# Spreading the variance of a LayerNorm over the partitions in one product

## The reference

```python
def layer_norm(x, g, b):
    xf = x.astype(F32)
    mu = jnp.mean(xf, axis=-1, keepdims=True)
    var = jnp.mean(jnp.square(xf - mu), axis=-1, keepdims=True)
    return ((xf - mu) * lax.rsqrt(var + EPS)).astype(x.dtype) * g + b

def conformer_conv(a, gt, w_dw, b_dw, ln_g, ln_b, w_pw):
    y = a * jax.nn.sigmoid(gt)
    y = lax.conv_general_dilated(y, w_dw[:, None, :], window_strides=(1,), ...) + b_dw
    return jax.nn.silu(layer_norm(y, ln_g, ln_b)) @ w_pw
```

## Time and profile before

| | us |
|---|---|
| median of 3 runs | 2111.23 |
| lowest and highest run | 2109.42 and 2115.57 |
| the profiled execution, its own time | 2113.24 |
| its span, first to last instruction | 2111.4 |
| PE busy | 1960.2 (93%) |
| DVE busy | 525.9 (25%) |
| ACT busy | 471.9 (22%) |

### The profile page before, as it was taken

How to read it: one execution, slowest core, us unless ns; L and a number is a source line. 1 busy time by engine, 2 the same in 40 slices (tenths; PEclk the granted TensorE clock), 3 DMA queues, 4 the chain that set the end, 5 groups by cost and what they waited for, 6 DMA issues and landing times.

```text
span 2111.4 us, 36634 instructions
## 1 busy us (share of the span) xinstructions
PE 1960.2 (93%) x15008; PEld 1099.3 (52%) x15008; DVE 525.9 (25%) x1193; ACT 471.9 (22%) x1031; POOL 150.5 (7%) x124
## 2 busy tenths in 40 slices
PE   5999999994999999999979999989879999999995
PEld 3756677882434444343456656778634443434342
DVE  1257122624111110111121841245421111111112
ACT  2232233222212111111131223332321111212112
POOL 0000001000010110101000000000001101011110
PEclk9999899996999999999989999999889999999998
DMA  9213123147899999999943122225449999999997
GB/s 307 84 58 120 41 81 103 68 175 285 327 390 393 385 394 389 390 393 390 388 143 119 64 80 80 68 76 207 171 179 384 392 391 390 392 390 394 386 397 250
DMA packets 210040, 533.78 MB, mean 253 GB/s; under 512 B 17072, under 2 KB 99376, under 8 KB 209712
## 3 DMA queue, kind: packets, MB, share of 16 engines
q1 hardware_dynamic: 191824, 493.52, 61.5%
q0 software_dynamic: 12288, 23.07, 5.1%
q10 hardware_dynamic: 5856, 16.16, 1.9%
HBM read 506.59 MB, written 26.12 MB: 252 GB/s over the span
## 4 chain that ended last, share of the span: by engine, by line
PE 68%; DMA 14%; SPq 8%; DVE 4%; issue 3%; ACT 2%; ACTq 0%; DVEq 0%; POOLq 0%
PE wide L1169 13%; DMA ring<-w_up 12%; PE wide L765 9%; PE wide L755 8%; PE wide L1177 7%; SPq L595 7%; PE wide L1047 7%; PE narrow L1200 6%; PE wide L1213 3%; PE turned L721 2%; PE wide L882 1%; PE narrow L701 1%; PE narrow L1070 1%; PE narrow L918 1%; PE wide L1188 1%
## 5 line engine op out<-in xcount | busy, mean ns | idle before, releaser
L1169 PE MATMUL wide<-ring,ht 128*64 128x512 f32 x2048 | 454.9, 599 | 9.5 <-DMA ring<-w_up 4.9
L1169 PEld LDWEIGHTS wide<-ring,ht 128*64 128x64 f32 x2048 | 143.7, 138 | 305.2 <-issue 278.5
L1177 PE MATMUL wide<-ring,ht 128*32 128x256 f32 x4096 | 234.3, 380 | 0.0
L1200 PE MATMUL narrow<-ring,ht 128*64 128x512 f32 x1024 | 233.8, 598 | 0.0
L2034 DVE TENSOR_TENSOR ht<-ht,wide 128x512 f32<-128x512 f32 x64 | 35.5, 554 | 680.4 <-ACT ht L1625 460.0
L765 PE MATMUL wide<-stream,ht 128*128 128x256 f32 (+1 forms) x960 | 192.4, 362 | 3.5 <-DVE ht L1704 3.5
L1177 PEld LDWEIGHTS wide<-ring,ht 128*32 128x32 f32 x4096 | 126.5, 110 | 108.2 <-issue 31.3
L765 PEld LDWEIGHTS wide<-stream,ht 128*128 128x128 f32 x960 | 169.4, 190 | 24.2 <-issue 4.0
L755 PE MATMUL wide<-ht,stream 128*128 128x128 f32 (+1 forms) x640 | 178.4, 441 | 0.0
L1625 ACT ACTIVATE ht<-wide 128x512 f32<-128x512 f32 x32 | 19.1, 597 | 623.4 <-PE wide L1169 623.4
L2200 POOL DMA_INDIRECT moe_sums<-ht x64 | 99.5, 1554 | 773.9 <-DVE ht L2051 695.5
(11 more groups left out here) (263 smaller groups left out, 1576.8 us busy)
## 6 DMA issues: line engine op xcount, KB each, us to landing
ring<-w_gate SPq DMA_DIRECT2D x256, 512.0 KB, 12.5
ring<-w_up SPq DMA_DIRECT2D x256, 512.0 KB, 14.1
ring<-w_down SPq DMA_DIRECT2D x128, 1024.0 KB, 19.7
stream<-w_mod SPq DMA_DIRECT2D x38, 1024.0 KB, 5.5
stream<-w_in SPq DMA_DIRECT2D x20, 1024.0 KB, 7.4
ring<-w_mod SPq DMA_DIRECT2D x10, 1024.0 KB, 12.0
stream<-w_out SPq DMA_DIRECT2D x6, 1024.0 KB, 5.9
moe_sums<-x ACTq DMA_DIRECT2D x10, 512.0 KB, 6.8
```

The costliest lines, as they stand in the source:

```text
L1169: ins = mm(psW[h * 64:(h + 1) * 64, 0, w * HALFW:(w + 1) * HALFW], xT[:, k, 0:CAPS], ring[:, k, w, h * HALFW:(h + 1) * HALFW], start=(k == ...
L1177: ins = mm(psW[q * STRIP:(q + 1) * STRIP, 1, w * QW:(w + 1) * QW], xT[:, k, CAPS:SLOTS], ring[:, k, w, q * QW:(q + 1) * QW], start=(k == 0 ...
L1200: ins = mm(psN[c * 64:(c + 1) * 64, 0, :], hmT[:, j, h_ * 64:(h_ + 1) * 64], ring[:, KD + k // 2, k % 2, c * HALFW:(c + 1) * HALFW], start ...
```

## The change: one product for the variance, reciprocal and root on full rows

The variance is now computed as the mean is: mean_w is stationary, the squares move, and the variance of a token stands in all 128 partitions of a wide bank. The narrow job var and the wide job cstd go; the wide job var stands where cstd stood. ACT takes the root of 128 x 640 values instead of 128 x 5 and writes it over the first chunk of csq, which frees the bank. DVE takes the reciprocal of these 640 values in place, links, and multiplies cscr by them out of SBUF; the signal s_crs now comes from this product and goes to ACT's Silu, not to PE. With one job less the narrow list has an even length, and its spare job goes too.

```diff
     elif _k == "conv_var":
-        N_JOBS += ["var"]
-        W_JOBS += ["cstd"]
+        W_JOBS += ["var"]
...
-DVE_LINKS = 148
+DVE_LINKS = 149
...
             def conv_var(l):
                 pe.wait_ge(s_csq, l + 1)
-                N.claim(pe, l, "var")
-                o = bank(N, "var")
-                for t in range(NT):
+                W.claim(pe, l, "var")
+                o = bank(W, "var")
+                for lo, hi in ((0, SAMPLE), (SAMPLE, NTOK)):
                     for c in range(NG):
-                        ins = mm(o[:, t:t + 1], csq[:, c, t * P:(t + 1) * P], mean_w[:, 0:1], start=(c == 0), stop=(c == NG - 1))
-                N.finish(ins)
-                pe.wait_ge(s_crs, l + 1)
-                W.claim(pe, l, "cstd")
-                o = bank(W, "cstd")
-                for t in range(NT):
-                    ins = mm(o[:, t * P:(t + 1) * P], crstd[:, t:t + 1].broadcast_to([P, P]), ident, start=True, stop=True)
+                        ins = mm(o[:, lo:hi], mean_w, csq[:, c, lo:hi], start=(c == 0), stop=(c == NG - 1))
                 W.finish(ins)
...
                     elif kind == "conv_var":
-                        out(N, l, "var", cstd, bank(N, "var")[:, 0:NT], ACT.Sqrt, bias=con("eps"))
-                        W.taken(act, l, "cstd")
+                        out(W, l, "var", csq[:, 0, :], bank(W, "var")[:, 0:NTOK], ACT.Sqrt, bias=con("eps"))
+                        act.wait_ge(s_crs, l + 1)
                         for c in range(NG):
                             A(zT[:, c, :], cscr[:, c, :], ACT.Silu, scale=par("lng")[:, c:c + 1], bias=par("lnb")[:, c:c + 1]).then_inc(s_z, 1)
...
             def conv_normalise(l):
-                N.taken(dve, l, "var")
-                V.reciprocal(crstd, cstd).then_inc(s_crs, 1)
-                W.wait(dve, l, "cstd")
-                W.take(V.tensor_tensor(cscr, cscr, bank(W, "cstd")[:, 0:NTOK].unsqueeze(1).broadcast_to([P, NG, NTOK]), ALU.mult), "cstd")
+                W.taken(dve, l, "var")
+                link(V.reciprocal(csq[:, 0, :], csq[:, 0, :]))
+                V.tensor_tensor(cscr, cscr, csq[:, 0, :].unsqueeze(1).broadcast_to([P, NG, NTOK]), ALU.mult).then_inc(s_crs, 1)
```

## The result

The changed kernel took 2115.85 us, median of 20 runs (2112.25 to 2119.37), against 2108.73 for the kernel before, also of 20 (2103.58 to 2118.86): a ratio of 1.0033, with a 95% interval of 1.0024 to 1.0042, or 7.0 us more, between 5.1 and 8.9. The profiled execution of the changed kernel took 2119.37 us with a span of 2117.6.

The account below looks back on a forecast made before the run. PE was taken as the bound, its first value product waiting, through ACT's copy of pt.1b, for DVE's product; 2 x (2.77 + 0.6) = 6.7 us more gave a median of 2117.9 us, range 2110.5 to 2123.0.

Parts of the forecast that it names:

- What decides is when DVE's product ends: DVE's product in conv_var: each microsecond later there is a microsecond later at PE's first value product, through ACT.
- The rival of the misplaced wait: First value product hangs on something other than pt.1b; at most 3.4 us gained in all, 2107.9; chance 0.05.
- The products of PE as the mean's, 2.28 us: PE in conv_var: four products shaped like the mean's take 2.28 us, replacing 2.36 and 1.70 us.
- The root at 0.79: ACT's root of 128 x 640 takes 0.79 us, like the exponential of the same shape.
- The long reciprocal from four short ones, 4.26 us: DVE's reciprocal of 640 elements per partition: line through four short sizes, 150 ns + 6.42 ns per element, 4.26 us.
- The flat rival: DVE's long reciprocal costs 0.82 us like any other operation; kernel not slower, 2110.7; chance 0.10.
- the steep one: DVE's long reciprocal takes 8.3 to 8.75 ns per element; 9 to 11.7 us more, 2120 to 2122.9; chance 0.20.
- 2.77 us per layer to the value product: DVE's product ends at 246.78 against 244.01, 2.77 us later per layer, passed undiminished by ACT to PE's first value product.
- 0.6 us of clock: PE behind its longer wait: low clock costs 0.6 us more per layer, bounds 0 and 1.6.
- Nothing for the rest: conv_out's later Silu, the spare job's removal, bank turns, SP's loads and POOL's work: no time won or lost.

Follow-up runs that it names:

- copy_first: The changed kernel with ACT's copy of pt.1b moved in front of its wait for DVE's product; measured 1.0015 of the kernel before.
- before_b: Second profile of the kernel before, nothing changed; the profiled execution took 2112.09 us.
- before_c: Third profile of the kernel before, nothing changed; the profiled execution took 2108.45 us.
- late_wide: The changed kernel with the whole step conv_var moved behind attention steps 3 to 5, ahead of the projection of rv; 0.9948 of the kernel before, then 0.9953.
- late_narrow: The kernel before with its own conv_var moved behind attention steps 3 to 5, ahead of the projection of rv; 0.9997 of the kernel before, then 1.0003.
- after_2: The changed kernel measured again, unaltered, on one chip with three others as their reference; 1.0045 of the kernel before.

## Why the prediction was right

The forecast, 2117.9 us or 6.7 more, was right in sign, size and mechanism. The time itself is 2.1 us lower, because the kernel before had a median of 2108.73 over 20 runs and not 2111.23 as over its first three; the difference, which the steps forecast, is 7.0. Its steps:

- *What decides is when DVE's product ends.* Shown: 4.19 us of wait per reciprocal (3.87, 8.06, 12.25), and a wait that is 2.59 us shorter and has another releaser when the copy of pt.1b is moved. The rival of the misplaced wait falls with copy_first. PE reached its wait even earlier than forecast, since it was granted 1.00 through the scores and turns; the wait took that up too, 8.06 us where 7 to 8 were expected.
- *The products of PE as the mean's, 2.28 us.* They took 2.28. *The root at 0.79.* It took 0.79.
- *The long reciprocal from four short ones, 4.26 us.* It took 4153 ns, 2.5% less. The flat rival (0.82) and the steep one (5.5 to 5.7) fall. That the line came so near is luck in part. It was drawn out to 53 times the largest of its sizes, and the four sizes do not rise evenly, though the prediction says so: from pair to pair the slope is 8.0, 2.3 and 8.75 ns per element, so that two of the three pairs, not one, spoke for the steep rival. The scatter of the four points leaves the slope uncertain by 0.8 ns (an estimate from these rows), which is 0.5 us at 640 elements. The trace of the kernel before had two more sizes, which the prediction did not use: 4 elements (168 to 179 ns) and 10 (209 ns). The line through all six is 6.2 ns per element, 4.1 us at 640. The Trainium skill's repeat count of 8 ("VectorE: DVE Perf Modes", First, the fixed hardware budget), read as 8 cycles per element, does not hold here: from 1 to 640 elements the cost rises by (4153 - 156) / 639 = 6.26 ns per element, and the measurement decides.
- *2.77 us per layer to the value product.* It was 2.64, smaller mainly by the reciprocal's 0.11.
- *0.6 us of clock.* It was 0.51, with PE at 1.2 GHz for 4.4 us, between the two stretches named. That is this pair of profiles; how near the term came is chance. In layer 0 of before_b and before_c the low clock came earlier, on the spreading products, and none came behind the first value product; conv_var with att:3 to att:5 took some 0.8 us less in all than in the first profile.
- *Nothing for the rest.* late_wide shows conv_out's cover for a much later Silu, and PE has no new wait for a bank in the stretch. What the spare job's removal is worth does not show: the time at its place varies between executions by 3.7 us (last section), and its product took 0.31.

The prediction put its forecast on the border between slower and no change, 0.3%, and gave both about half; the interval, 1.0024 to 1.0042, holds that border too.

What it did not ask is whether conv_var had to stand there at all. On the way from the first product of conv_var to the end of DVE's product the change took 1.78 us of PE's products away (2.36 + 1.70 against 2.28) and put 3.96 us of DVE and 0.52 of ACT in; in the early place all of that stands before PE's first value product. In the late place DVE's and ACT's share lies beneath the projection and only PE's share and PE's own waits count, and there the same form of conv_var beats the short reciprocal by half a percent (0.9948 against 0.9997, again 0.9953 against 1.0003).

## What to carry to other kernels

Where in-order engines share one list, as here, a step's price shows at what stands behind it in the queues: find the first thing that the bottleneck waits for behind it, and put a step that is needed late behind that. Moving alone is not enough: it paid in the form in which PE does not wait in the middle of the step (late_wide), and not in the other (late_narrow). Two forms of a step are compared in the place where it will stand; here the order of the two turned round with the place. And a short instruction that grows with its length where its neighbours are at their floor can give the price of the long one: fit all the sizes that the trace has, and state how far their scatter lets the line swing.

## What had not been expected

The granted clock differs between executions of one kernel at the same place: 0.57 and 0.76 between 210 and 217 us in two profiles of the kernel before, 0.54 and 1.00 in two of the changed one, whose stretch from the mean to conv_out took 73.9 and 70.5 us in layer 0. At the end of the dense half of layer 0, the time from the products of line 1148, behind the turned tables, to the first expert was 12.5, 12.3 and 8.8 us in three profiles of the kernel before. A single profile therefore places a stage to a few microseconds only, and sums from it are best made inside a stretch, from one event to another, as 10.40 against 13.04 above. Even so, the 10.40 was 11.20 and 11.21 in layer 0 of before_b and before_c, and the 13.04 came again in both layers of after_2: one more profile of each kernel is worth its price.

In the kernel before, PE fell to 1.2 GHz behind its one-column products and the wait for the reciprocal: the granted clock was 1.00 from 237.8 to 240.8 us and 0.50 from 242.4 to 244.4. In the changed kernel it was still granted 1.00 there, while it went from products of 512 columns to scores; what in the one-column products or the wait lets the clock fall was not tested:

```profile
241.00:244.40 3.40, 1.39 (x7) 0.72 (x5) 3.40 (x1) 0.81 (x1) 0.00 (x0) 1.00 0.17 56
```

The higher clock was worth nothing early, where PE ran into the wait.
